# Two transformer blocks in one program: later totals of weight chunks, and the second norm's first work moved beside the projection

## The reference, cut to what matters

```
def first_block(x, ...):
    x = layer_norm(x, ln_in_g, ln_in_b)
    h = x @ w_in                       # 1024 -> 2816 columns, split into ten parts
    y = concat(spatial gating, conformer conv, window attention)   # 1024 columns
    return layer_norm(DEEPNORM_ALPHA * x + y @ w_out, post_ln_g, post_ln_b)

def second_block(x, ...):
    h = rmsnorm(x, norm_pre_g)         # x * rsqrt(mean(x*x) + 1e-6) * g
    z = h @ w_in                       # 1024 -> 4096 columns: q, k, v, gates, conv inputs
    q, k = rope(q), rope(k)
    o = three dilated window attentions, mixed by their log-sum-exp
    mixed = concat(o * silu(g_attn), gated causal conv)
    return x + rmsnorm(mixed @ w_out, norm_post_g)
```

## Time and profile before

| | |
|---|---|
| median of 3 runs | 2297.74 us (2291.33 to 2300.5) |
| profiled execution, its own time | 2291.84 us |
| its span, first to last instruction | 2289.7 us |
| mean granted TensorE clock | 0.962 |
| TensorE busy | 2082.4 us (91% of the span) |
| VectorE busy | 1394.7 us (61%) |
| ScalarE busy | 923.1 us (40%) |
| GpSimd busy | 906.7 us (40%) |

### The profile page before, as it was taken

One profiled execution on the slowest core, in us unless ns is written; L12 is line 12 of the kernel. 1 busy time (PEld: TensorE's weight loads), 2 busy tenths in 40 slices (PEclk: granted clock), 3 DMA queues, 4 the chain that ended last, 5 costly groups with the idle time before them and its releaser, 6 DMA issues.

```text
span 2289.7 us, 43310 instructions
## 1 busy us (share of the span) xinstructions
PE 2082.4 (91%) x16228; PEld 1525.7 (67%) x16228; DVE 1394.7 (61%) x3507; ACT 923.1 (40%) x1981; POOL 906.7 (40%) x1004
## 2 busy tenths in 40 slices
PE   5999999997898999499999999999988888887998
PEld 3545868886787888488644444656877766666786
DVE  7614949765897444773376772213179999994422
ACT  3323333222796000232233431211179999883111
POOL 4311333363422999332111211211132888983222
PEclk9999999998899999799999999999999999997999
DMA  5441321346633232442344431321156787674552
GB/s 180 134 110 57 108 80 44 92 142 201 154 80 107 79 109 98 156 135 66 115 118 137 117 116 49 117 73 55 49 123 161 195 197 185 169 220 135 161 172 90
DMA packets 285536, 279.95 MB, mean 122 GB/s; under 512 B 39712, under 2 KB 237216, under 8 KB 285072
## 3 DMA queue, kind: packets, MB, share of 16 engines
q1 hardware_dynamic: 281280, 271.08, 41.1%
q0 software_dynamic: 1680, 5.51, 0.6%
q10 hardware_dynamic: 2368, 0.60, 0.1%
HBM read 171.22 MB, written 93.31 MB: 116 GB/s over the span
## 4 chain that ended last, share of the span: by engine, by line
PE 27%; DVE 16%; issue 4%; ACT 2%; POOL 2%; DMA 2%; SPq 1%; DVEq 0%; ACTq 0%; POOLq 0%
PE bank L172 19%; PE bank L2507 7%; DVE s2m L2357 6%; DVE p2l L2363 4%; DMA qr<-qf 1%; DVE qf L1801 1%; SPq L1830 1%; ACT s2sh L1781 1%; DVE qr L1799 1%; DVE s2sl L1804 1%; DVE qf L1798 1%; DVE ob L2369 1%; PE bank L2302 1%; POOL qs L2399 0%; ACT p2r L2336 0%
## 5 line engine op out<-in xcount | busy, mean ns | idle before, releaser
L172 PE MATMUL bank<-xh,w2l 128*128 128x512 f16 x640 | 244.7, 382 | 0.0
L172 PE MATMUL bank<-xh,w2h 128*128 128x512 f16 x640 | 244.5, 382 | 0.0
L172 PE MATMUL bank<-xl,w2h 128*128 128x512 f16 x640 | 244.5, 382 | 0.0
L172 PE MATMUL bank<-w1h,xh 128*128 128x256 f16 x768 | 212.6, 277 | 3.0 <-DVE s1st L918 3.0
L172 PE MATMUL bank<-w2h,xh 128*128 128x256 f16 x768 | 211.3, 275 | 2.0 <-issue 2.0
L2302 PE MATMUL bank<-ident,p2r 128*128 128x128 f32 x900 | 165.9, 297 | 51.9 <-DVE p2l L2363 45.7
L172 PE MATMUL bank<-w1l,xh 128*128 128x256 f16 x768 | 212.5, 277 | 0.0
L172 PE MATMUL bank<-w1h,xl 128*128 128x256 f16 x768 | 212.4, 277 | 0.0
L172 PE MATMUL bank<-w2h,xl 128*128 128x256 f16 x768 | 211.2, 275 | 0.0
L172 PE MATMUL bank<-w2l,xh 128*128 128x256 f16 x768 | 211.2, 275 | 0.0
L2302 PEld LDWEIGHTS bank<-ident,p2r 128*128 128x128 f32 x900 | 97.4, 145 | 108.5 <-DVE p2l L2363 105.7
(11 more groups left out here) (345 smaller groups left out, 5643.1 us busy)
## 6 DMA issues: line engine op xcount, KB each, us to landing
scr_part<-ob SPq DMA_DIRECT2D x48, 264.0 KB, 3.2
cm<-scr_part SPq DMA_DIRECT2D x48, 264.0 KB, 4.7
v<-scr_v SPq DMA_DIRECT2D x192, 65.0 KB, 2.6
w2r<-in_w_in SPq DMA_DIRECT2D x12, 1024.0 KB, 6.4
qr<-qf SPq DMA_DIRECT2D x192, 64.0 KB, 2.0
ax<-in_x SPq DMA_DIRECT2D x16, 512.0 KB, 5.3
xr<-in_x SPq DMA_DIRECT2D x16, 512.0 KB, 4.4
bx<-scr_x SPq DMA_DIRECT2D x16, 512.0 KB, 6.2
```

What stands on the lines that cost most here:

```text
L172: ins = nc.tensor.matmul(dst, x, y, start=k == 0 and m == 0, stop=k == n - 1 and m == 2)
```

## The change

In the norms the third chunk's total moves from behind the first chunk's second group to behind its third group, the fourth chunk's total from before the third chunk's first group to behind it, and ScalarE's scaling of the fourth chunk one group later. In the gates the next chunk's total moves from the second to the fourth tile, on VectorE with it, and ScalarE's scaling from before the fifth tile to before the sixth (in loop indices from `m % 8` of 1, 2 and 4 to 3, 4 and 5).

The second norm's head moves into the projection: SyncE loads the first chunk at tile 6 and the first four row tiles at tiles 8 to 11; VectorE works out the scale at tiles 5, 8 and 11, the rows' statistics at tiles 10 to 14 and scales the rows at tile 15; GpSimd has three operations at tile 10 and the power at tile 14; TensorE has the scale's one-column matmul at tile 7, into a bank of the transposes' four, taken between the eighth and ninth tiles' banks (counted from zero) and released by VectorE at tile 8. These buffers lie on the right side of SBUF until the norm ends. In the second norm every engine but TensorE now waits for the projection's end first. The raw weights of the first chunk have a buffer of their own (`raw_of`), so the third chunk's load no longer waits for the first chunk's split. The pad that kept the second norm's tiles clear of the projection's is gone.

The diff, cut to its core (the lines that only replace `raw[n % 2]` by `raw_of(n)` and the new semaphores are left out):

```diff
@@ -195,10 +196,11 @@
             self.total = [(self.d_t, self.d_t.n + n + 1) for n in range(len(chunks))]
             self.scaled = [(self.g_u, self.g_u.n + 5 * n + 5) for n in range(len(chunks))]
             self.landed, self.by_act, self.half, self.ready = [], [], [], []
+            self.first = first
             for n, c in enumerate(chunks):
-                dma_at[n % 2] += 16 * len(c["cols"])
+                dma_at[n % 2] += 16 * len(c["cols"]) if n or first is None else 0
                 at[1] += 1
-                self.landed.append((self.dma[n % 2], dma_at[n % 2]))
+                self.landed.append((self.dma[n % 2], dma_at[n % 2]) if n or first is None else first[1])
                 self.by_act.append((self.a_w, at[1]))
                 if c["fast"]:
                     at[2] += 1
...
 
+        def raw_of(self, n):
+            return self.first[0] if n == 0 and self.first is not None else self.raw[n % 2]
+
         def sp_load(self, n):
             if n >= len(self.chunks):
                 return
-            if n > 1:
+            if n > (1 if self.first is None else 2):
                 sp.wait_ge(*self.ready[n - 2])
                 if n - 2 in self.read:
                     sp.wait_ge(*self.read[n - 2])
             at = 0
             for c, k in self.chunks[n]["cols"]:
...
@@ -311,11 +317,11 @@
         d_bd, d_vs = sem("d_bd"), sem("d_vs")
         vt, vh = heads
         d_wd, d_gs, g_wd, g_xh, p_wd = sem("d_wd"), sem("d_gs"), sem("g_wd"), sem("g_xh"), sem("p_wd")
-        if late:
-            sb(f"{tag}pad", [128, 17000], scope=scope)
         block = 1 if late else 0
         own, whole = wide[:, 2 * block:2 * block + 1], wide[:, 2 * block + 1:2 * block + 2]
-        wts.widened = d_gs.at(1)
+        wts.widened = ahead["widened"] if late else d_gs.at(1)
+        fitted_at = ahead["fitted"] if late else d_gs.at(2 if shift is None else 3)
+        off = 1 if late else 0
         splits = [wts.chunks[n]["kind"][0] == "f" for n in range(3)]
         if any(splits):
             hbuf, lbuf = sbs(f"{tag}sh", 2, [128, 512], FR, scope), sbs(f"{tag}sl", 2, [128, 512], FR, scope)
...
@@ -327,16 +333,16 @@
         if turned:
             vf = sbs(f"{tag}vf", 2, [128, 512], F32, scope)
         p_vt, a_vf = sem("p_vt"), sem("a_vf")
-        n_most = 2 if shift is None else 3
+        n_most = 0 if late else 3
         for k, n in enumerate(valued):
             wts.read[n] = d_bd.at(n_most + 3 * k + 1)
-        xs = sbs(f"{tag}x", 4, [128, D], F32, scope)
+        xs = ahead["rows"] if late else sbs(f"{tag}x", 4, [128, D], F32, scope)
         xf = sbs(f"{tag}f", 4, [128, 512], F32, scope)
         st = sb(f"{tag}st", [128, 4, 12], scope=scope)
         mv = sb(f"{tag}mv", [128, 4, 2], scope=scope)
         rs = sb(f"{tag}rs", [128, 4], scope=scope)
...
@@ -351,19 +357,21 @@
                     work.append(("turn_v", g - 1))
             work.append(("group", 0, g))
             if g == 1:
-                work += [("load", 2), ("total", 2)]
+                work.append(("load", 2))
+            if g == 2:
+                work.append(("total", 2))
         work += [("split", 2), ("group", 1, 3)]
         if turned:
             work.append(("turn_v", 3))
-        work += [("consts",), ("load", 3), ("total", 3)]
-        work += [("group", 2, 0), ("scaled", 3)] + [("group", 2, g) for g in range(1, 4)]
+        work += [("consts",), ("load", 3)]
+        work += [("group", 2, 0), ("total", 3), ("group", 2, 1), ("scaled", 3), ("group", 2, 2), ("group", 2, 3)]
 
         bk = Banks(range(8))
         turn_bank, v_bank, steps, n_mm, n_split, n_val = {}, {}, {}, 0, 0, 0
         total_bank, bound_bank = {}, {}
         for item in work:
             if item[0] == "wide":
-                wide_bank = bk.take(g_wd.at(0) if False else d_wd.at(3))
+                wide_bank = bk.take(d_wd.at(3))
             elif item[0] == "total":
                 total_bank[item[1]] = bk.take(wts.total[item[1]])
             elif item[0] == "turn":
...
@@ -423,7 +429,7 @@
                 dve_most()
                 dve_widest()
             dve.wait_ge(*d_st.now())
-            dve.wait_ge(*g_pw.at(g + 1))
+            dve.wait_ge(*g_pw.at(g + 1 - off))
             for t in range(4):
                 if keep:
                     nc.vector.tensor_scalar(xs[t][:], xs[t][:], m_out[:, t:t + 1], r_out[:, t:t + 1], ALU.subtract, ALU.mult).then_inc(*d_sc.up())
...
@@ -597,14 +603,10 @@
             dve.wait_ge(*d_vs.now())
 
         def dve_program():
-            if not keep:
-                dve_most()
-                dve_widest()
+            take_over(dve)
+            if not late:
+                dve_scale(0)
                 dve_widened()
-            dve_scale(0)
-            if keep:
-                dve_widened()
-            take_over(dve)
             for item in work:
                 if item[0] == "total":
                     wts.dve_total(item[1], total_bank[item[1]][0])
...
@@ -679,9 +679,10 @@
                     wts.pool_scale(item[1])
 
         def sp_program():
-            sp_fetch(0)
             take_over(sp)
-            wts.sp_load(0)
+            if not late:
+                sp_fetch(0)
+                wts.sp_load(0)
             wts.sp_load(1)
             for item in work:
                 if item[0] == "load" and item[1] > 1:
...
@@ -1539,6 +1545,66 @@
             for h in range(2):
                 t_bank[n, h] = tbk.take(d_yl.at(2 * n + h + 1))
                 m_bank[n, h] = mbk.take(d_z.at(2 * n + h + 1))
+            if n == 8:
+                wide_bank = tbk.take(d_wd.at(5))
+
+
+        def sp_ahead(n):
+            if n == 6:
+                nc.sync.dma_start(raw2[:], w2.rearrange("(t p) n -> p t n", p=128)[:, :, cols2:cols2 + 256]).then_inc(*w_in.up(16))
+            if 8 <= n < 12:
+                t = n - 8
+                sp.wait_ge(*x_out[t].at(16))
+                nc.sync.dma_start(rows2[t][:], x1[128 * t:128 * t + 128, :]).then_inc(*n_in[t].up(16))
+
+        def dve_ahead(n):
+            if n == 5:
+                dve.wait_ge(*REST)
+                nc.vector.scalar_tensor_tensor(most[:, 0, :], g2T[:], -1.0, g2T[:], ALU.mult, ALU.max).then_inc(*d_wd.up())
+                dve.wait_ge(*d_wd.now())
+                nc.vector.tensor_scalar(most[:, 0, :], most[:, 0, :], float(D) ** 0.5, None, ALU.mult).then_inc(*d_wd.up())
+                dve.wait_ge(*d_wd.now())
+                nc.vector.tensor_tensor(most[:, 1, :], most[:, 0, :], most[:, 0, :], ALU.mult).then_inc(*d_wd.up())
+                dve.wait_ge(*d_wd.now())
+                nc.vector.tensor_reduce(own, most[:, 1, :], mybir.AxisListType.X, ALU.add).then_inc(*d_wd.up())
+            elif n == 8:
+                dve.wait_ge(*p_wd.at(1))
+                nc.vector.tensor_scalar(whole, wide_bank[0][:, 0:1], 1e-30, None, ALU.max).then_inc(*d_wd.up())
+            elif n == 11:
+                dve.wait_ge(*g_wd.at(3))
+                nc.vector.tensor_scalar(whole, whole, 1.0 / HTOP, None, ALU.mult).then_inc(*d_gs.up())
+                nc.vector.tensor_scalar(fitted[:, 0, :], g2T[:], own, None, ALU.mult).then_inc(*d_gs.up())
+            if 10 <= n < 14:
+                t = n - 10
+                dve.wait_ge(*n_in[t].at(16))
+                for h in range(2):
+                    nc.vector.bn_stats(st2[:, t, 6 * h:6 * h + 6], rows2[t][:, 512 * h:512 * h + 512]).then_inc(*d_sx.up())
+                dve.wait_ge(*d_sx.now())
+                nc.vector.bn_aggr(mv2[:, t, :], st2[:, t, :]).then_inc(*d_sx.up())
+            elif n == 14:
+                mean, var = mv2[:, :, 0], mv2[:, :, 1]
+                dve.wait_ge(*d_sx.now())
+                nc.vector.tensor_tensor(rs2[:], mean, mean, ALU.mult).then_inc(*d_sx.up())
+                dve.wait_ge(*d_sx.now())
+                nc.vector.tensor_tensor(rs2[:], rs2[:], var, ALU.add).then_inc(*d_sx.up())
+                dve.wait_ge(*d_sx.now())
+                nc.vector.tensor_scalar(rs2[:], rs2[:], RMS_EPS, None, ALU.add).then_inc(*d_sx.up())
+            elif n == 15:
+                dve.wait_ge(*g_nx.at(1))
+                for t in range(4):
+                    nc.vector.tensor_scalar(rows2[t][:], rows2[t][:], rs2[:, t:t + 1], None, ALU.mult).then_inc(*d_nx.up())
+
+        def pool_ahead(n):
+            if n == 10:
+                pool.wait_ge(*d_wd.at(5))
+                nc.gpsimd.tensor_tensor(own, whole, power[:, 0:1], ALU.pow).then_inc(*g_wd.up())
+                pool.wait_ge(*g_wd.now())
+                nc.gpsimd.tensor_tensor(whole, whole, own, ALU.mult).then_inc(*g_wd.up())
+                pool.wait_ge(*g_wd.now())
+                nc.gpsimd.tensor_scalar(own, own, HTOP, None, ALU.mult).then_inc(*g_wd.up())
+            elif n == 14:
+                pool.wait_ge(*d_sx.at(15))
+                nc.gpsimd.tensor_tensor(rs2[:], rs2[:], power[:, 0:4], ALU.pow).then_inc(*g_nx.up())
 
         def pe_turn(n):
             for h in range(2):
```

(43 more changed lines are left out.)

35 lines of the change are left out of this document (16 added, 19 removed).

## The result

The changed kernel takes 2261.81 us (median of 4 runs, 2258.81 to 2262.78), the kernel before beside it 2296.85 (2291.33 to 2300.50). The ratio is 0.985, with an interval of 0.983 to 0.987: 35 us less. The forecast was 2268.5 in a range of 2260 to 2283. Two later comparisons of the same pair gave 0.9865 (0.985 to 0.988) and 0.986 (0.984 to 0.988), 30.7 and 32.8 us; so 31 to 35 us is what stands.

What follows compares the result with a forecast made beforehand. TensorE's in-order queue held up by waits for small totals, half-clock stretches behind them, and the second norm's front: 7.1 + 7.4 + 8.65 + 6.05 = 29.2 us off the 2297.74 median gives 2268.5 us, range 2260 to 2283.

Steps and rivals of the forecast that it cites:

- Totals of the first norm: First norm: two moved totals save TensorE waits of 2.67 and 2.72 us plus a 1.72 us half-clock stretch, 7.11 us.
- Totals of the second norm: Second norm: two moved totals save waits of 2.76 and 2.67 us plus half-clock stretches of 1.72 and about 1.5, 8.65 us.
- Gates: Gates: the first moved total saves its 4.34 us TensorE wait and the 1.72 us half-clock stretch behind it, 6.06 us.
- The cover of 7 us: Gates: GpSimd's later subtraction for the next chunk still ends 7 us before TensorE starts that chunk.
- Front: Second norm's start: ScalarE squares 6.67 us earlier, VectorE's second remainder comes 0.75 us nearer, together 7.4 us.
- bare it would be about 3 us: Projection's last tile: VectorE's 2.74 us row scaling counted as nothing, hidden by a 2.98 us wait for TensorE; uncovered about 3 us.
- The store's landing: Projection's end: the last store takes 2.9 us without the row loads, instead of 6.27; 6.3 kept for the range.
- The stop in the projection: Projection's tenth turn, second half: TensorE waits 1.7 us for a transpose bank; with 0.43 for one-column matmuls, 2.1 us.
- Stretches stay: Rival: TensorE's half-clock stretches behind the totals remain, so only 22.5 us is saved, 2275 us; chance 0.18.
- The front keeps its length: Rival, second norm's start: slow 6.3 us store landing leaves a gain of 2.3 us or nothing; 2274 to 2276 us, chance 0.12.
- The totals wait again: Rival, moved totals: ScalarE's squaring stands behind evictions of the groups put ahead; 2290 us, no change, chance 0.06.
- The gates' next chunk is late: Rival, gates: chunk preparation ends after TensorE wants it, in six chunks; 14 us later gives 2310 us, slower; chance 0.04.

Runs made afterwards that it cites:

- Late scaling: Changed kernel with VectorE's scaling of the four rows moved behind its last projection tile; 0.985 twice against the kernel before, 2260.7 and 2260.8 us.
- rope's: Late scaling kernel with rope's one-column bound sum asked behind the chunk's first tile; 0.985 against the kernel before, 2262.7 us beside 2260.8 for its base.

## Why the prediction was right, and where it was off

The mechanism held for all four parts, and the sum of their places, from the table's means, is 8.3 + 4.0 + 8.8 + 8.1 = 29.2 us against a predicted 29.2. That is luck in part: the first norm and the gates gave 3.2 us more than predicted, the front 3.4 less, and the two errors cancel.

*Totals of the first norm*, predicted 7.11, measured 348.5 - 340.2 = 8.3. The stretch behind the first total was counted as none, since the earlier trace rows showed none; it is there in two of five profiles. The three without it still have a mean of 348.1, 7.9 above, so most of the difference stays open.

*Totals of the second norm*, predicted 8.65, measured 136.9 - 128.1 = 8.8.

*Gates*, predicted 4.34 + 1.72 = 6.06, measured 44.4 - 36.3 = 8.1. Wait and stretch are both longer in other profiles (5.44 us, and a clock of 0.50 over the whole of the 4 us read). Even in the profile that the prediction read the place is 43.7 - 36.3 = 7.4 us longer, so 1.3 us of the difference stays open. The cover of 7 us was as worked out.

*Front*, predicted 7.4, measured 4.0. The step that failed is the one that counted the scaling at nothing, with "bare it would be about 3 us": its cover, the 2.98 us that the last addition waits for TensorE, holds only for operations of 2.74 us. Beside GpSimd they took 6.99, and the last addition came late. Late scaling gives 7.4 (244.5 - 237.1, the mean of three profiles with it, rope's among them), which is what was predicted for free operations, though not by the predicted terms alone: there ScalarE squares 4.0 us behind the store's issue (3.05 in the prediction), and from the squaring to the first eviction it takes 1.1 us less than before (0.75 in the prediction). The store's landing, taken as 2.9, was 3.76 from issue to SyncE and 4.01 to ScalarE; the bound of 6.3 that the range kept did not come. The stop in the projection was taken as 1.7 and is 0 to 1.3.

The Trainium skill, "SBUF — State Buffer", section "SBUF: two separate sides", says that VectorE and GpSimd share a pair of ports, which the one that starts first holds for a whole instruction while the other waits; VectorE wants them for an operation in a mode that uses both its ports, or for one with two inputs from this memory against a GpSimd operation that reads it. The traces agree: 6.99 us beside GpSimd and 2.73 us alone for the same four operations, and a 128x4 product that lasts as long as GpSimd's operation beside it (below). The prediction did not weigh this rule; by it the scaling would have been priced at its own 2.74 and GpSimd's two operations of 2.4, at most 7.5 us (an estimate from these rows). That product in the timelines of VectorE and GpSimd, in the changed kernel:

```profile
899.03 2.39 DVE L1589 TENSOR_TENSOR rsN<-rsN,mvN 128x4 f32<-128x4 f32 x1
...
899.00 2.40 POOL L1713 TENSOR_TENSOR xr<-xr,bcpg 128x1024 f32<-128x1024 f32 x1 [0.93 <-DVE xr L1661]
```

*The base.* The forecast stood 6.7 us above the median measured, because the whole of the 5.9 us between the profiled execution and the median was carried over to the changed kernel. Part of it, 2.2 us by the second profile, lay in the very stretches and waits that the change removes. Between 29.2 us of places and 31 to 35 us of medians some 2 to 6 us are left. Stretches come and go in parts that the change does not touch (from conv's eviction of the table to the projection's first turn 378.7 to 384.3 us over all profiles, from rope's first eviction to its last 248.2 to 254.6), and whether the change has a share in that was not settled. In the means of two profiles before and three of the changed kernel the parts not touched are 2.7 us shorter, nearly all of it between conv's eviction and the projection (382.2 against 379.4).

*The rivals.* "Stretches stay" is out: none stood behind the five totals in three profiles of the changed kernel. "The front keeps its length" was half right (4.0 us, between its 2.3 and the predicted 7.4), by another mechanism than the one given: not the landing, but the work put ahead of the last tile. "The totals wait again" came true for one total in rope, where another wait was moved. "The gates' next chunk is late" is out by the 7.0 us of cover.

## What to carry to other kernels

Ask for a small result where its producer has long been done, and price such a wait as its length and the half-clock stretch that mostly stands behind it; where a wait can't be moved, work that nobody reads may pay for itself. Before work is put beside other work "for nothing", look at what the neighbour engine does in those microseconds, not only at whether the engine itself is idle: four operations worth 2.7 us cost 3.2 us of the end, and nothing one step later. Take the worth of an edit from the length of its own place in several profiles, since a single execution may have been spared, or hit, at just the spot that the edit removes.

## What was not expected of the hardware

Small operations are not always small beside GpSimd. Ten beside the projection were counted at about 0.15 us each, and in the changed kernel's profile four of them, the 128x4 product above among them, took 2.2 to 2.4 us while a GpSimd operation ran. The other six took 0.15 to 0.17 us, though a GpSimd operation ran beside most of these too, and the statistics beside GpSimd kept their 0.7 us; which operations are held up was not tried. The four were covered: in the projection TensorE waits for VectorE nowhere but at the stop. And dense matmuls that nobody reads, put into an idle wait of TensorE, made the program 9.6 us faster.
